# A hybrid decoder layer on one core: transposed attention weights through two PSUM regions, and a new order of work on ScalarE and VectorE

## Chip, core and metric

The kernel runs on one core of a Trainium2 chip. The metric is device time in microseconds (us). Matrix products run on TensorE (PE in the profile; PEld is its weight load), and the rest on VectorE (DVE), ScalarE (ACT), GpSimd (POOL) and the DMA queues.

## What is computed

One decoder layer for 1024 prompt tokens and 8 sequences of 4 new tokens: four mixers after one input projection, an output projection, a gated MLP, a gated embedding. The two attention mixers matter here:

```python
s = einsum('bqhd,bsd->bqhs', qi, ki); score = einsum(relu(s), wi) * IDX_SCALE
_, sel = lax.top_k(score, n_sel)                                   # "dsa": the 256 best keys
a = softmax(q @ k[sel] * 64**-0.5); y_c = a @ v[sel]
a = softmax(q1 @ k1 * 32**-0.5) - lam * softmax(q2 @ k2 * 32**-0.5)  # "diff"
y_d = rmsnorm(a @ v) * (1 - lam_init)
```

## The kernel before

The attention is cut into items, one for each query tile i (128 tokens) and head h: "diff" and "dsa" for the prompt, "sdiff" and "sdsa" for the new tokens. `ITEMS` lists them in order; position n in it is called step n, and each step has four places p = 0 to 3. Between the pieces of an item, each engine does its share of "dense" work: the projections, and from step 37 the MLP of the first 384 tokens, at a fixed number of products for each place. Steps 39 to 62 hold the diff items of tiles 3 to 7, with an sdiff item after each of the first four tiles (steps 43, 48, 53, 58), and steps 63 to 86 the dsa items. In steps 39 to 60 there also runs the search for the 256th largest score, bit by bit: in a stage, VectorE forms a candidate (L1338), then VectorE counts three arrays (L1288) and ScalarE three others (L1357), and VectorE's next stage begins by reading both (L1324). Most stages stand at places 1 and 3 up to step 49, at 2 and 3 in steps 52 and 53, and at 1 and 2 in steps 55 to 59.

An item goes through these pieces. Step n, place 0: PE makes the logits (L1507, sdiff L1517), VectorE adds the mask and takes the maximum (`dve_maxima`, L1787, L1796; ends with L1805), ScalarE takes the exponentials (`act_exp`, L1644). Place 3: VectorE combines the two maps (`dve_finish`, L1814 to L1817). Step n+1, places 2 and 3: PE transposes the weights in chunks of up to four 128-column blocks (`pe_transposes`, L1578, sdiff L1582) into PSUM bank 4, and ScalarE copies each chunk out (`act_transposed`, L1687, sdiff L1689). Step n+2, place 1: PE multiplies by the values (`pe_outputs`, L1550) into bank 5, whose halves serve two tiles in turn. Once a tile has its four heads, VectorE reads it at step n+3, place 0 (`dve_tile`, L1844 to L1850, with a power on POOL, L1944), PE transposes the result at n+4, place 1 (L1602), and ScalarE copies it (L1674).

All uses of bank 4 stand in one list, `USES`: chunks ("tr"), a tile's result ("y"), products for the samples ("so", transposed back as "sot", L1594) and some small ones. PE may write for use k only when ScalarE has copied use k-1:

```python
def pe_use(pe, use):
    k = USE_OF[use]
    if k:
        pe.wait_ge(use_cp, k)
```

ScalarE at a step: place 0 the exponentials of n; place 1 copies of sample and tile results, then its counts; place 2 the first chunk of n-1, then counts; place 3 the second chunk, then counts. VectorE: place 0 `dve_tile(n-3)` and maxima; places 1 and 2 stages; place 3 `dve_finish`, then a stage. The dense pieces (gate's tanh L905 on ScalarE, its product L958 on VectorE, the MLP sum L950 on VectorE) stand between them. Weights are fetched by SP's queue.

Of the kernel before, what the change touches and what calls it, by code (L numbers as in the profile page):

```python
# [7 lines left out]
P = 128  # L8
# [356 lines left out]
def chunks(n):  # L365
    kind, i, h = ITEMS[n]
    return {"none": 0, "sdiff": 2, "sdsa": 1}.get(kind, (i + 4) // 4)
# [6 lines left out]
USES = []  # L374
for n in range(NN):
    if n >= 2 and ITEMS[n - 2][0] in ("sdiff", "sdsa"):
# [8 lines left out]
USE_OF = {use: k for k, use in enumerate(USES)}  # L385
TR_OF = {use: sum(a[0] != "so" for a in USES[:k]) for k, use in enumerate(USES)}


def build(nc, d):
# [4 lines left out]
    with ExitStack() as ctx:  # L394
# [123 lines left out]
        def bank(j):  # L518
            return ps8[:, j]

# [219 lines left out]
        def tile_no(n):  # L740
            return sum(item[0] in PROMPT for item in ITEMS[:n]) // 4

# [351 lines left out]
        def pe_use(pe, use):  # L1094

            k = USE_OF[use]
            if k:
                pe.wait_ge(use_cp, k)

        def pe_misc(pe, use):  # L1100
            pe_use(pe, use)
            kind = use[0]
            if kind == "v":
# [3 lines left out]
                for j, slot in enumerate((DV, DV + 1, CV)):  # L1107
                    last = nc.tensor.transpose(bank(4)[0:w, j * P:(j + 1) * P], Z[:, slot, cols], c_("ident"))
            if kind == "maps":
# [5 lines left out]
                last = nc.tensor.matmul(bank(4)[:, 0:w], early_("maps")[:, c * P:(c + 1) * P], H[:, PV + c, cols], start=True, stop=True)  # L1115
            if kind == "wcol":
                pe.wait_ge(s_early, 16)
                for g in range(2):
                    last = nc.tensor.matmul(bank(4)[:, 8 * g:8 * g + 8], early_(f"e{g}", NS), ctok[0:NS, QT, HD:HD + 8], start=True, stop=True)
            if kind == "dsum":  # L1120
                pe.wait_ge(dsq, 1)
                last = nc.tensor.matmul(bank(4)[:, 0:64], c_("headones"), osqs[:, :], start=True, stop=True)
            last.then_inc(tr_mm, 1)

        def act_misc(act, use):
            kind = use[0]
            act.wait_ge(tr_mm, TR_OF[use] + 1)
            if kind == "v":
                t = use[1]
                w = P if t < QT else NS  # L1130
                nc.scalar.activation(dtok[0:w, t], bank(4)[0:w, 0:256], ACT.Copy)
                last = nc.scalar.activation(ctok[0:w, t], bank(4)[0:w, 256:328], ACT.Copy)
            if kind == "maps":
                c, half = use[1:]
                cols = part_a if half == 0 else slice(NA + (half - 1) * CB, NA + half * CB)
                last = nc.scalar.activation(H[:, PV + c, cols], bank(4)[:, 0:cols.stop - cols.start], ACT.Copy, scale=p_("pool_scale")[:, c:c + 1])
            if kind == "wcol":
                last = nc.scalar.activation(wcp, bank(4)[:, 0:16], ACT.Copy)
            if kind == "dsum":
                last = nc.scalar.activation(omean[:, :], bank(4)[:, 0:64], ACT.Identity, bias=eps[:, :], scale=1.0 / HD)  # L1140
# [396 lines left out]
        def pe_outputs(pe, n):  # L1537
# [3 lines left out]
            pe.wait_ge(use_cp, USE_OF["tr", n, chunks(n) - 1] + 1)  # L1541
            pt = probs_t(n)
            if kind in PROMPT:
                tile = tile_no(n)
                if h == 0 and tile:
                    pe.wait_ge(o_read, tile)
                for b in range(i + 1):
                    v = dtok[:, b, HD * h:HD * h + HD] if kind == "diff" else ctok[:, b, 0:HD]
                    at = 256 * (tile % 2) + HD * h
                    last = nc.tensor.matmul(bank(5)[:, at:at + HD], pt[:, b * P:(b + 1) * P], v, start=b == 0, stop=b == i)  # L1550
            else:
                pe_use(pe, ("so", n))
                if kind == "sdiff":
                    pe.wait_ge(dv_in, 16 * 2 * NPG * (i + 1))
                    for g in range(NPG + 1):
                        rows = P if g < NPG else NS
                        for b in range(2):
                            v = pair_values[b][:, g] if g < NPG else dtok[0:NS, QT, 0:256]
                            last = nc.tensor.matmul(bank(4)[32 * b:32 * b + 32, 0:256], pt[0:rows, g * 64 + 32 * b:g * 64 + 32 * b + 32], v,
                                                    start=g == 0, stop=g == NPG)  # L1560
                for c in range(2 if kind == "sdsa" else 0):
                    for g in range(NPG + 1):
                        rows = P if g < NPG else NS
                        v = dsa_values(i, c)[:, g] if g < NPG else ctok[0:NS, QT, 0:HD]
                        out, p = bank(4)[0:HD, c * 16:c * 16 + 16], pt[0:rows, g * 32 + c * 16:g * 32 + c * 16 + 16]
# [3 lines left out]
        def pe_transposes(pe, n, c):  # L1569
# [5 lines left out]
            pe_use(pe, ("tr", n, c))  # L1575
            if kind in PROMPT:
                for b in range(4 * c, min(4 * c + 4, i + 1)):
                    last = nc.tensor.transpose(bank(4)[:, (b % 4) * P:(b % 4 + 1) * P], logits(n)[:, b * P:(b + 1) * P], c_("ident"))  # L1578
            elif kind == "sdiff":
                for g in (range(5, NPG + 1) if c else range(5)):  # L1580
                    w = P if g < NPG else NS
                    last = nc.tensor.transpose(bank(4)[0:w, (g - 5 * c) * 64:(g - 5 * c) * 64 + 64], logits(n)[0:64, g * P:g * P + w],  # L1582
                                               c_("ident", 64)[:, 0:64])
            else:
                for g in range(NPG + 1):
                    w = P if g < NPG else NS
                    last = nc.tensor.transpose(bank(4)[0:w, g * 32:g * 32 + 32], logits(n)[0:32, g * P:g * P + w], c_("ident", 32)[:, 0:32])
            last.then_inc(tr_mm, 1)

        def pe_sample_back(pe, n):  # L1590

            pe_use(pe, ("sot", n))
            for c in range(2):
                last = nc.tensor.transpose(bank(4)[:, 64 * c:64 * c + 64], so_rows[0:64, c * P:(c + 1) * P], c_("ident", 64)[:, 0:64])  # L1594
            last.then_inc(tr_mm, 1)

        def pe_tile(pe, n):
            if ends_tile(n):
                pe.wait_ge(yt_ready, tile_no(n) + 1)
                pe_use(pe, ("y", n))  # L1600
                for j in range(2):
                    last = nc.tensor.transpose(bank(4)[:, j * P:(j + 1) * P], yt[:, j * P:(j + 1) * P], c_("ident"))  # L1602
# [30 lines left out]

        def act_exp(act, n):
# [12 lines left out]
        def act_sample(act, n):  # L1647
# [4 lines left out]
            if kind == "sdiff":  # L1652
                last = nc.scalar.activation(so_rows[0:64, :], bank(4)[0:64, 0:256], ACT.Copy)
            else:
                o = bank(4)[0:HD, 0:32].rearrange("p (b h t) -> p h b t", b=2, h=4)
# [5 lines left out]
        def act_sample_back(act, n):  # L1661
# [3 lines left out]
                                 bank(4)[:, 0:128].rearrange("p (c b r) -> p c b r", c=2, b=2), ACT.Copy).then_inc(use_cp, 1)  # L1665
# [1206 lines left out]
```

## Time and profile before

| | |
|---|---|
| three runs | 1782.15, 1775.49, 1781.06 us; median 1781.06 |
| span of the profiled execution | 1784.0 us |
| PE busy | 1641.7 us (92%) |
| VectorE busy | 1120.8 us (63%) |
| ScalarE busy | 684.7 us (38%) |
| GpSimd busy | 215.2 us (12%) |

No time outside the span is given for the profiled execution, so its span is its time here; it lies 2.9 us above the median of the runs. An engine's share is an average over stages with different limits, so the stretches of the span are to be read one by one. A row's arrow names what the idle time before an instruction ended on; "issue" is idle time for which the profile shows no wait.

### The profile page before, as it was taken

What the parts mean: (1) busy time and instruction counts of PE and PEld (TensorE: products, weight loads), DVE (VectorE), ACT (ScalarE), POOL (GpSimd) and SP (SyncE); (2) the same over time, 40 slices, a digit from 0 to 9 for tenths busy, and PEclk for the clock granted to TensorE, in tenths of its full rate; (3) what the DMA queues carried; (4) which work ended last, traced back from release to release, by engine and by line L of the source; (5) the groups of instructions that cost most, each with busy time, mean ns of one, the idle gap of its engine ahead of it and who ended that gap; (6) DMA issues with size and microseconds to landing.
All of it is one profiled execution on the core that took longest, in us unless ns stands there. A gap on an engine that the chain in (4) does not pass through costs nothing.

```text
span 1784.0 us, 26755 instructions
## 1 busy us (share of the span) xinstructions
PE 1641.7 (92%) x9433; PEld 1400.4 (78%) x9433; DVE 1120.8 (63%) x2415; ACT 684.7 (38%) x1273; POOL 215.2 (12%) x360
## 2 busy tenths in 40 slices
PE   6989998998978798889999999999999999999996
PEld 5978898873534454456787799899999999999995
DVE  6466856277788887776656555566555555556845
ACT  5333443354367366532333333342222222222531
POOL 1000000031313322063322001000000000000000
PEclk9999999998989898899998999999999999999997
DMA  5331122141523323132322223122222222222312
GB/s 192 118 106 48 60 78 72 62 160 61 175 74 118 104 92 107 49 106 94 92 75 73 72 83 138 53 83 86 72 71 71 71 71 71 71 71 77 106 60 110
DMA packets 52815, 158.32 MB, mean 89 GB/s; under 512 B 9776, under 2 KB 13872, under 8 KB 52704
## 3 DMA queue, kind: packets, MB, share of 16 engines
q1 hardware_dynamic: 37840, 121.37, 20.2%
q0 software_dynamic: 14864, 35.53, 6.3%
q8 instruction: 62, 1.02, 0.2%
q14 instruction: 49, 0.40, 0.1%
HBM read 147.10 MB, written 9.76 MB: 88 GB/s over the span
## 4 chain that ended last, share of the span: by engine, by line
PE 57%; DVE 11%; issue 8%; ACT 5%; POOLq 1%; POOL 1%; DMA 0%; DVEq 0%; ACTq 0%
PE ps L2077 22%; PE ps L832 15%; PE ps L2264 9%; ACT act_junk L1357 2%; PE ps L1550 2%; DVE junk_b L1288 2%; DVE Pb_b L1787 2%; PE ps L1507 1%; PE ps L2438 1%; PE ps L1578 1%; PE ps L1162 1%; DVE SC L1194 1%; ACT Pb_b L1644 1%; DVE wl L581 1%; ACT wh L574 1%
## 5 line engine op out<-in xcount | busy, mean ns | idle before, releaser
L581 DVE TENSOR_TENSOR wl<-wr,wh 128x1024 fp32r<-128x1024 f32 x176 | 215.4, 1224 | 284.0 <-ACT wh L574 283.4
L574 ACT ACTIVATE wh<-wr 128x1024 fp32r<-128x1024 f32 x176 | 186.0, 1057 | 424.0 <-PE ps L2077 221.1
L2077 PE MATMUL ps<-xh_b,wh 128*128 128x336 f32 x960 | 305.4, 318 | 7.4 <-DVE wl L581 3.3
L2077 PE MATMUL ps<-xl_b,wh 128*128 128x336 f32 x960 | 305.7, 318 | 0.0
L2077 PE MATMUL ps<-xh_b,wl 128*128 128x336 f32 x960 | 303.9, 317 | 0.0
L2077 PEld LDWEIGHTS ps<-xh_b,wh 128*128 128x128 f32 x960 | 181.8, 189 | 8.9 <-DVE wl L581 4.0
L2077 PEld LDWEIGHTS ps<-xh_b,wl 128*128 128x128 f32 x960 | 181.8, 189 | 0.0
L2077 PEld LDWEIGHTS ps<-xl_b,wh 128*128 128x128 f32 x960 | 181.3, 189 | 0.0
L832 PE MATMUL ps<-x_a,wr 128*128 128x384 f32 x384 | 152.9, 531 | 1.7 <-DVE H L950 1.7
L832 PE MATMUL ps<-xh_a,wh 128*128 128x384 f32 x400 | 141.2, 353 | 8.3 <-ACT Z L873 3.0
L1644 ACT ACTIVATE Pb_b<-Pb_b,tiny 128x512 f32<-128x512 f32 (+6 forms) x68 | 65.2, 959 | 201.2 <-DVE tiny L1805 201.2
L832 PE MATMUL ps<-xl_a,wh 128*128 128x384 f32 x400 | 139.4, 349 | 0.0
L832 PE MATMUL ps<-xh_b,wh 128*128 128x336 f32 x352 | 114.9, 326 | 0.8 <-ACT Z L873 0.8
L832 PE MATMUL ps<-xl_b,wh 128*128 128x336 f32 x352 | 115.2, 327 | 0.0
L832 PE MATMUL ps<-xh_b,wl 128*128 128x336 f32 x352 | 114.5, 325 | 0.0
L1288 DVE TENSOR_SCALAR_CACHE_REDUCE junk_b<-SC,tk_b 32x1056 uint16<-32x1056 uint16 (+7 forms) x105 | 107.5, 1024 | 6.8 <-DMA SC<-score_spill 3.3
L2264 PE MATMUL ps<-al_b,wh 128*128 128x336 f32 x352 | 111.6, 317 | 0.0
L2264 PE MATMUL ps<-ah_b,wh 128*128 128x336 f32 x352 | 111.3, 316 | 0.2 <-DVE H L2348 0.2
L2264 PE MATMUL ps<-ah_b,wl 128*128 128x336 f32 x352 | 111.3, 316 | 0.0
L832 PEld LDWEIGHTS ps<-x_a,wr 128*128 128x128 f32 x384 | 71.1, 201 | 50.0 <-issue 19.3
L2348 DVE TENSOR_TENSOR H<-H,ps 128x336 f32<-128x336 f32 x176 | 85.1, 502 | 33.2 <-PE ps L2264 31.4
L1357 ACT ACTIVATE act_junk<-SC,tk_b 128x1024 bf16<-128x1024 uint16 (+2 forms) x93 | 93.4, 1004 | 9.9 <-DVE tk_b L1338 7.4
(420 smaller groups left out, 3174.1 us busy)
## 6 DMA issues: line engine op xcount, KB each, us to landing
wr<-in_weights SPq DMA_DIRECT2D x212, 512.0 KB, 3.4
pages<-in_d_pages POOLq DMA_DIRECT2D x64, 128.0 KB, 2.4
values<-in_d_pages POOLq DMA_DIRECT2D x64, 128.0 KB, 2.4
pages<-in_c_pages POOLq DMA_DIRECT2D x128, 32.0 KB, 2.1
H<-in_xT SPq DMA_DIRECT2D x8, 336.0 KB, 8.6
H<-in_xT POOLq DMA_DIRECT2D x8, 336.0 KB, 5.8
out_y<-Y_out_b SPq DMA_DIRECT2D x8, 336.0 KB, 2.3
H<-in_xT SPq DMA_DIRECT2D x8, 192.0 KB, 4.9
```

The source lines that it names most:

```text
L574: nc.scalar.activation(wh[:, slot], wr[:, slot], ACT.Copy).then_inc(w_hi, 1)
L581: nc.vector.tensor_tensor(wl[:, slot], wr[:, slot], wh[:, slot].bitcast(f32), ALU.subtract).then_inc(w_lo, 1)
L832: last = nc.tensor.matmul(out[:, cols], w, x, start=j == 0, stop=j == count - 1)
L1162: last = nc.tensor.matmul(bank(2 * (u % 2) + h)[:, 0:w], Z[r, QI + p, i * P:(i + 1) * P], Z[r, KI2, a:a + w], start=True, stop=True)
L1288: return nc.vector.tensor_scalar(self.junk[0:rows, 0:S], src, scalar, 0.0, op, ALU.add, accum_out=self.col(CNT, j, rows))
L1357: nc.scalar.activation(out[:, 0:S], self.half(j, k >= 15), ACT.Sign, bias=self.col(NBIAS, j), accum_out=self.col(CNT, j)).then_inc(self.ac ...
L1550: last = nc.tensor.matmul(bank(5)[:, at:at + HD], pt[:, b * P:(b + 1) * P], v, start=b == 0, stop=b == i)
L1644: last = nc.scalar.activation(p, p, ACT.Exp, bias=nm[0:rows, col:col + 1], scale=SCALE[kind], accum_out=sm[0:rows, col:col + 1])
L1787: last = nc.vector.tensor_tensor_reduce(out=logits(n, m)[:, 0:S], in0=src[:, 0:S], in1=mask, scale=1.0, scalar=-3e38, op0=ALU.add, op1=ALU ...
L2077: last = nc.tensor.matmul(bank(first_bank + c)[:, 0:CB], w, x, start=k == 0 and t == 0, stop=k == KC - 1 and t == 2)
L2264: last = nc.tensor.matmul(down_bank(v), w, x, start=q == 0 and t == 0, stop=q == 1 and t == 2)
L2348: nc.vector.tensor_tensor(cols, cols, down_bank(v), ALU.add).then_inc(h_ffn, 1)
```

## The change

Tiles 6 and 7 are transposed in three chunks of 4, 2 and 2 (or 1) blocks; tiles 4 and 5 stay at two. The uses are sorted into two kinds. "Narrow" ones (so, y, wcol, dsum, and every second chunk) go to the upper half of bank 5, and the others stay in bank 4. A use waits for the previous use of its own kind. Values products now use only the lower half of bank 5, and since PE must not write a bank while another engine reads it, a narrow use also waits until VectorE has read all tiles multiplied before it, and values products wait until earlier narrow uses are copied. `pe_outputs` waits chunk by chunk. The third chunk is transposed and copied at the end of place 3, after the dense work. On ScalarE, the exponentials move from place 0 to place 2, behind the copy of the first chunk. On VectorE, `dve_tile` (and POOL's power) moves from place 0 of the third step to place 2 of the second, ahead of that place's stage, and at place 3 the stage comes before `dve_finish`.

```diff
-    return {"none": 0, "sdiff": 2, "sdsa": 1}.get(kind, (i + 4) // 4)
+    return {"none": 0, "sdiff": 2, "sdsa": 1}.get(kind, 1 if i < 4 else 2 if i < 6 else 3)
+
+def blocks(n, c):
+    i = ITEMS[n][1]
+    return range(*((0, min(4, i + 1)), (4, min(6, i + 1)), (6, i + 1))[c])
...
-        USES += [("tr", n - 1, c) for c in range(chunks(n - 1))]
+        USES += [("tr", n - 1, c) for c in range(min(2, chunks(n - 1)))]
     if n >= 2 and ITEMS[n - 2][0] == "sdiff":
         USES.append(("sot", n - 2))
+    if n >= 1 and chunks(n - 1) == 3:
+        USES.append(("tr", n - 1, 2))
...
+def narrow(use):
+    return use[0] in ("so", "y", "wcol", "dsum") or use[0] == "tr" and use[2] == 1
...
+        def use_at(use):
+            return ps8[:, 5, 256:512] if narrow(use) else ps8[:, 4]
...
         def pe_use(pe, use):
-            k = USE_OF[use]
-            if k:
-                pe.wait_ge(use_cp, k)
+            if BEFORE[use] >= 0:
+                pe.wait_ge(use_cp, BEFORE[use] + 1)
+            read = tiles_before(use) if narrow(use) else 0
+            if read:
+                pe.wait_ge(o_read, read)
...
         # pe_outputs
+                if NARROW_BEFORE[n]:
+                    pe.wait_ge(use_cp, NARROW_BEFORE[n])
                 for b in range(i + 1):
+                    for c in range(chunks(n)):
+                        if b == blocks(n, c)[0]:
+                            pe.wait_ge(use_cp, USE_OF["tr", n, c] + 1)
...
         # act_mixers
             if p == 0:
-                act_exp(act, n)
...
                 if n:
                     act_transposed(act, n - 1, 0)
+                act_exp(act, n)
                 act_stage(act, n, 2)
...
         # dve_mixers
             if p == 0:
-                if n >= 3:
-                    dve_tile(dve, link, n - 3)
                 dve_maxima(dve, link, n)
...
             if p == 2:
+                if n >= 2:
+                    dve_tile(dve, link, n - 2)
                 dve_stage(dve, link, n, 2)
...
             if p == 3:
+                dve_stage(dve, link, n, 3)
                 dve_finish(dve, link, n)
-                dve_stage(dve, link, n, 3)
...
         # scalar; the same with pe_transposes on PE
                 act_dense(act, place)
+                if place % 4 == 3 and third_chunk(place // 4):
+                    act_transposed(act, place // 4 - 1, 2)
```

## Rows read from the trace of the kernel before

**Rows 1.** The page: span, and busy time of each engine.

```profile
span 1784.0 us, 26755 instructions
PE 1641.7 (92%) x9433; PEld 1400.4 (78%) x9433; DVE 1120.8 (63%) x2415; ACT 684.7 (38%) x1273; POOL 215.2 (12%) x360
```

**Rows 2.** Windows: length; PE, PEld, DVE, ACT, POOL busy (count); granted clock; DMA; GB/s.

```profile
0.00:450.00 450.00, 403.72 (x2325) 348.26 (x2325) 275.77 (x699) 189.84 (x376) 40.88 (x71) 0.97 0.29 97
...
510.00:767.00 257.00, 213.66 (x919) 115.09 (x920) 204.25 (x509) 142.97 (x290) 61.59 (x110) 0.89 0.29 94
767.00:1062.00 295.00, 274.82 (x1558) 219.92 (x1557) 175.68 (x355) 107.57 (x206) 76.13 (x120) 0.95 0.25 78
...
522.00:528.00 6.00, 6.00 (x15) 2.85 (x14) 5.06 (x14) 3.71 (x8) 0.61 (x1) 0.50 0.01 3
```

**Rows 3.** Waits of PE, 510 to 767 us: total, times, longest.

```profile
PE ps L1582 <- ACT PT_b L1689: 17.7, 4, 8.8
PE ps L1578 <- ACT PT_b L1687: 11.8, 8, 3.2
PE ps L1578 <- ACT H L1674: 6.7, 2, 4.9
PE ps L1594 <- ACT PT_b L1687: 4.6, 4, 3.1
```

**Rows 4.** Waits of PE, 767 to 1062 us.

```profile
PE ps L832 <- issue: 10.9, 9, 3.2
PE ps L1578 <- ACT H L1674: 5.5, 1, 5.5
```

**Rows 5.** Waits of PE, 0 to 450 us.

```profile
PE ps L1578 <- ACT H L1674: 2.5, 2, 1.8
```

**Rows 6.** Waits of VectorE, 510 to 767 us.

```profile
DVE tk_b L1324 <- ACT act_junk L1357: 13.4, 9, 2.7
DVE gv_a L958 <- ACT ge_a L905: 8.7, 5, 2.4
DVE Pb_b L1796 <- PE ps L1517: 5.8, 2, 3.1
...
DVE Pb_b L1787 <- PE ps L1507: 4.3, 1, 4.3
...
DVE tiny L1814 <- ACT Pb_b L1644: 2.0, 1, 2.0
DVE H L950 <- PE ps L832: 1.9, 1, 1.9
```

**Rows 7.** Timeline of step 51: start, duration, instruction, idle before it.

```profile
618.34 0.17 DVE L1805 TENSOR_SCALAR tiny<-tiny 128x2 f32<-128x2 f32 x1
618.54 0.93 ACT L1644 ACTIVATE Pb_b<-Pb_b,tiny 128x768 f32<-128x768 f32 x1 [9.52 <-DVE tiny L1805]
...
620.39 0.51 ACT L905 ACTIVATE ge_a<-gv_a 128x384 f32<-128x384 f32 x1
620.80 0.60 ACT L1674 ACTIVATE H<-ps,subln 128x128 f32<-128x128 f32 x2
...
621.55 1.09 PE L1578 MATMUL ps<-cst,Pb_b 128*128 128x128 f32 x4 [4.93 <-ACT H L1674]
```

**Rows 8.** Timeline of step 44, sdiff transposed.

```profile
520.15 0.75 DVE L1288 TENSOR_SCALAR_CACHE_REDUCE junk_b<-SC,tk_b 128x512 uint16<-128x512 uint16 x1
...
521.02 0.42 ACT L1689 ACTIVATE PT_b<-ps 128x320 f32<-128x320 f32 x1
...
521.49 0.68 PE L1582 MATMUL ps<-cst,Pb_b 64*128 64x64 f32 x4 [8.75 <-ACT PT_b L1689]
```

**Rows 9.** Groups by shape: count, busy, mean ns, idle before.

```profile
L1687 ACT ACTIVATE PT_b<-ps 128x256 f32<-128x256 f32 x8 | 3.0, 378 | 7.3 <-PE ps L1578 7.3
L1844 DVE TENSOR_TENSOR ot<-ps,tiny 128x256 f32<-128x256 f32 x8 | 3.3, 416 | 0.0
L1817 DVE SCALAR_TENSOR_TENSOR Pb_b<-Pb_b,tiny 128x768 f32<-128x768 f32 x4 | 4.1, 1019 | 0.1
```

**Rows 10.** Timeline: a stage at place 3, read after `dve_finish` (step 52).

```profile
638.32 0.17 DVE L1324 TENSOR_TENSOR tk_b<-tk_b 128x12 f32<-128x12 f32 x1 [1.51 <-ACT act_junk L1357]
```

**Rows 11.** Timeline: a weight load after a wait already met.

```profile
651.33 0.94 PEld L832 LDWEIGHTS ps<-gu_a,wr 128*128 128x128 f32 x4 [0.55 <-issue]
```

More of the change, by code:

```diff
@@ L381 @@
     if n >= 1:
-        USES += [("tr", n - 1, c) for c in range(chunks(n - 1))]
+        USES += [("tr", n - 1, c) for c in range(min(2, chunks(n - 1)))]
     if n >= 2 and ITEMS[n - 2][0] == "sdiff":
         USES.append(("sot", n - 2))
+    if n >= 1 and chunks(n - 1) == 3:
+        USES.append(("tr", n - 1, 2))
 USE_OF = {use: k for k, use in enumerate(USES)}
+def narrow(use):
+    return use[0] in ("so", "y", "wcol", "dsum") or use[0] == "tr" and use[2] == 1
+BEFORE = {use: max((j for j in range(k) if narrow(USES[j]) == narrow(use)), default=-1) for k, use in enumerate(USES)}
+NARROW_BEFORE = {n: sum(1 for use in USES[:k] if narrow(use)) and 1 + max(j for j in range(k) if narrow(USES[j])) for n, k in USES_BEFORE.items()}
 TR_OF = {use: sum(a[0] != "so" for a in USES[:k]) for k, use in enumerate(USES)}
@@ L741, in tile_no, with tiles_before @@
             return sum(item[0] in PROMPT for item in ITEMS[:n]) // 4
+        def tiles_before(use):
+            k = USE_OF[use]
+            return tile_no(1 + max(n for n, first in USES_BEFORE.items() if first <= k))
         def diff_tiles(n):
@@ L1114, in pe_misc @@
                 w = cols.stop - cols.start
-                last = nc.tensor.matmul(bank(4)[:, 0:w], early_("maps")[:, c * P:(c + 1) * P], H[:, PV + c, cols], start=True, stop=True)
+                last = nc.tensor.matmul(use_at(use)[:, 0:w], early_("maps")[:, c * P:(c + 1) * P], H[:, PV + c, cols], start=True, stop=True)
             if kind == "wcol":
@@ L1575, in pe_transposes @@
             pe_use(pe, ("tr", n, c))
+            dst = use_at(("tr", n, c))
             if kind in PROMPT:
-                for b in range(4 * c, min(4 * c + 4, i + 1)):
-                    last = nc.tensor.transpose(bank(4)[:, (b % 4) * P:(b % 4 + 1) * P], logits(n)[:, b * P:(b + 1) * P], c_("ident"))
+                for at, b in enumerate(blocks(n, c)):
+                    last = nc.tensor.transpose(dst[:, at * P:(at + 1) * P], logits(n)[:, b * P:(b + 1) * P], c_("ident"))
             elif kind == "sdiff":
@@ L1581, in pe_transposes @@
                     w = P if g < NPG else NS
-                    last = nc.tensor.transpose(bank(4)[0:w, (g - 5 * c) * 64:(g - 5 * c) * 64 + 64], logits(n)[0:64, g * P:g * P + w],
+                    last = nc.tensor.transpose(dst[0:w, (g - 5 * c) * 64:(g - 5 * c) * 64 + 64], logits(n)[0:64, g * P:g * P + w],
                                                c_("ident", 64)[:, 0:64])
@@ L1586, in pe_transposes @@
                     w = P if g < NPG else NS
-                    last = nc.tensor.transpose(bank(4)[0:w, g * 32:g * 32 + 32], logits(n)[0:32, g * P:g * P + w], c_("ident", 32)[:, 0:32])
+                    last = nc.tensor.transpose(dst[0:w, g * 32:g * 32 + 32], logits(n)[0:32, g * P:g * P + w], c_("ident", 32)[:, 0:32])
             last.then_inc(tr_mm, 1)
@@ L1632, in pe_mixers, with third_chunk @@
                     pe_sample_back(pe, n - 2)
+        def third_chunk(n):
+            return n >= 1 and chunks(n - 1) == 3
         def act_exp(act, n):
@@ L1839, in dve_tile @@
             heads = lambda x: x.rearrange("p (h d) -> p h d", d=HD)
-            o = heads(bank(5)[:, 256 * (tile % 2):256 * (tile % 2) + 256])
+            o = heads(bank(5)[:, 0:256])
             a = 4 * (tile % 2)
@@ L2696, in _ @@
                 pe_dense(pe, place)
+                if place % 4 == 3 and third_chunk(place // 4):
+                    pe_transposes(pe, place // 4 - 1, 2)
             pe_out(pe)
```

61 lines of the change are left out of this document (31 added, 30 removed).

## The prediction

> **What bounds the kernel now.** I read the page first: PE is busy 92% of the span, no other engine more than 63% [rows 1]. That average hides different stages, so I cut the span into windows [rows 2]. From 0 to 450 us and from 1062 us on, the change touches little. Between 510 and 767 us, where the search runs beside the diff items, PE is busy 213.7 of 257 us although its mean granted clock is only 0.89, and VectorE 204.3 us. Neither is full: the two hold each other up. From 767 to 1062 us PE is busy 274.8 of 295 us and sets the pace.
>
> Then I read the waits. In the search stretch PE waits 17.7 us for the first sdiff chunk's copy, 11.8 us for a first prompt chunk's, 6.7 us for a tile's, 4.6 us before the samples are transposed back: 40.8 us, all for ScalarE to empty bank 4 [rows 3]. The timeline of step 51 shows why ScalarE is late. It meets the exponentials first and stands before them for 9.52 us until VectorE's maxima; then they take 1.85 us (618.54 to 620.39), then come tanh and the tile's copy; PE has idled 4.93 us [rows 7].
>
> But PE's idle time is not the price. VectorE is nearly a second bound here, and PE, freed, meets it again. So I cost this stretch by VectorE's waits: 13.4 us for ScalarE's counts, 8.7 us for tanh, 5.8 and 4.3 us for logits from a late PE, 2.0 us for exponentials, 1.9 us for the MLP product [rows 6].
>
> **The change part by part, search stretch.**
>
> *ScalarE's counts before the exponentials.* In steps with a stage at place 1, ScalarE now counts at once instead of 1.85 us later [rows 7]. Of nine waits totalling 13.4 us, seven are in such steps, and I take 1 us from each: 7 us gained. Bounds: nothing, and all 13.4 us.
>
> *Tanh not behind the exponentials.* Tanh stands directly behind them in steps 44 and 51 ([rows 7] shows the second). Two of the five waits, each near the longest, 2.4 us [rows 6], go: 4.6 us. Bounds 0 and 8.7.
>
> *PE no longer waits for bank 4.* The second chunk and the tile's result have a region of their own, so the 11.8 and 6.7 us [rows 3] go, and the samples' way back waits only for the first chunk: most of 4.6 us. What VectorE gets of these 23 us is its waits for logits, 5.8 and 4.3 us, and for the MLP product, 1.9 us: 12.0 us in all [rows 6]. The stalls ahead are about as long (longest 3.2, 3.1 and 4.9 against 3.1, 4.3 and 1.9), so I take 10.7. Bounds 0 and 12.0.
>
> *The sdiff stall of 17.7 us mostly stays.* At the step after an sdiff item, a tile has just been multiplied. The sdiff second chunk is narrow, so PE must wait for VectorE to read that tile, at place 2, behind the stage of place 1. In step 44 that stage's last count starts at 520.15 and takes 0.75 us, so the read (0.416 us [rows 9]) would end near 521.4; ScalarE's copy today frees PE at 521.49, after 8.75 us [rows 8]. The wait changes its name. It costs VectorE nothing, as VectorE is the one that is late. I take no gain. The Trainium skill ("PSUM — Partial Sum Buffer", PSUM bank collisions) says that PSUM must be guarded by bank and quadrant, not by address, because engines in disjoint columns of one bank collide; by that rule these waits can't be left out, and by a guard on addresses alone the 17.7 us of PE would go too. No row shows a collision.
>
> *`dve_finish` behind the stage.* Finishing now waits for nothing at step 50: 2.0 us gained [rows 6]. But in steps 52 and 53, with stages at places 2 and 3, finishing stood between VectorE's counts and its wait for ScalarE's. Even so 1.51 us were left to wait [rows 10]. Without that cover its time, 1.0 us for the combination [rows 9] and some 0.5 us of small operations, is waited: 2 x 1.6 = 3.2 us lost. ScalarE's tanh of step 53 now stands behind exponentials started later: 1.5 us lost. Combined weights come up to one stage later at steps 44 to 53, but PE uses them two places into the next step.
>
> *`dve_tile` moved.* The same five operations and POOL's power, once a tile: nothing. At place 2 it waits for PE's place 1, where PE is mostly ahead.
>
> *Third chunks.* 16 more copies at no more than 0.378 us [rows 9]: 6 us on ScalarE, busy 143 of 257 us [rows 2], hidden. Should that cover go, they cost 6 us.
>
> Sum here: 7 + 4.6 + 10.7 + 2.0 - 3.2 - 1.5 = 19.6 us gained.
>
> **From 767 us.** At 773 us PE waits 5.5 us for a tile's copy [rows 4], the tile ending in step 58, and from there PE sets the pace: this goes entirely. PE's clock had dropped to 0.50 after such a stall, with PE then busy throughout (522 to 528 us [rows 2]); a few us of work at half speed go too, 1.5 us. Gain 7.0. The other large wait there, 10.9 us on dense products [rows 4], is about operands, which the change leaves.
> New waits: values products of tiles 4 to 7 stop for the second and third chunk, 24 times among the dsa items (8 once, 8 twice). Met waits elsewhere delay a weight load by up to 0.55 us while PE's products go on [rows 11]; so between 0 and 13 us; I take 0.1 us each, 2.4, as products are queued ahead. After each dsa tile PE's second chunk waits for VectorE's read, four times, behind one mask stage at place 1; PE has two places of dense work before it. Between 0 and 1.0 us each; I take 0.5, 2 us in all.
>
> **Before 450 us.** Of two waits of 2.5 us for a tile's copy [rows 5], all goes; with small ones, 3 us. PE sets the pace there.
>
> **Total.** 19.6 + 7.0 + 3 - 2.4 - 2 = 25.2 us from the profiled 1784.0 us: 1758.8. That execution lies 2.9 us above the median of the runs, so I predict 1756 us, a ratio of 0.986.
>
> **The rivals.**
>
> *More than that, 1730 (chance 0.10).* With 23 of 40.8 us of stalls gone, PE hardly drops to the low clock, and pulls VectorE along. At a mean clock of 0.89, PE spends 22% of 257 us, 57 us, at half speed [rows 2]; half of that time is loss. If most of it matters, 25 us more. Against it: VectorE's 204 us plus its own latencies leave it little room.
>
> *VectorE is the bound and nothing comes back but the edge, 1774 (0.19).* PE runs ahead, then waits for maxima, or for values' chunks, and ScalarE's counts at place 2 are now behind the exponentials, so VectorE waits there instead. Then 19.6 shrinks to about 0, and 7.0 + 3 - 4.4 = 5.6 remain, within half a per cent of no change. For it: the sdiff case above, where one wait takes another's place. Against it: after the stage at place 2, VectorE still has finishing and the next maxima to do before it reads ScalarE's counts.
>
> *Slower, 1796 (0.12).* The place is `dve_finish` behind the stage at place 3. Combined weights come later by VectorE's counts, some 3.6 us, in about ten steps; where PE already stands at the transposes, it idles for as long and its clock then falls to 0.50 as it did at 522 us [rows 2]. Ten such stalls with as much lost again at half speed are 70 us of PE's time; PE has 257 - 213.7 = 43.3 us of idle time to lend [rows 2], of which about 15 stay in the sdiff stalls, so 42 us of loss less the 25 gained. It decides once PE arrives less than 3.6 us after finishing, in half or more of the steps. The Trainium skill ("TensorE: Matmul & The Clock Gate", Part 1) says that throttled is the default state and only activity releases it; by that rule each new long stall is followed by slow products, as at 522 us, and this case would give the 1796.
> Against it: PE reaches the transposes two places into the next step, and today waits there for ScalarE, hardly ever for VectorE.
>
> *The forecast, 1756 (0.59).* Its own range, from the bounds: 1742 to 1768.
>
> **How the numbers follow.** Half a per cent is 9 us, about what a measurement of this kernel can tell from no change. The forecast and the first rival are faster by more than that, and a little of the second: 0.59 + 0.10 + 0.02 = 0.71. Same: 0.17 of the second and a little of the slow case, 0.18. Slower: 0.11. The range for 8 in 10 leaves out the slow case's greater part and most of the first rival: 1738 to 1785.
>
> **What would show it.** L1578 waits for PT_b and for H gone from PE's list between 510 and 767 us; L1582 waiting about as long, now for VectorE (ot, L1844's successor); VectorE's wait for ScalarE's counts at 6 to 7 us instead of 13.4; that stretch shorter by some 20 us; no stall of PE near 773 us; mean clock above 0.89. It is wrong if PE's waits for combined weights grow past 10 us, if VectorE waits for exponentials or counts as long as before, or if values products show gaps between chunks.

## Result, and the profile after

| | before | changed |
|---|---|---|
| median of the runs on the same chip | 1780.65 us | 1756.46 us |
| lowest and highest | 1775.49, 1782.15 | 1745.55, 1759.72 |
| profiled execution | 1784.0 (its span) | 1758.01 (span 1756.3) |

The ratio is 0.987, 95% interval 0.9834 to 0.9906: faster, by 24 us or 1.3%, with the whole interval below 1. I had predicted 1756 us. The total is right. The working is only partly so. In the search stretch two of its terms missed by more than 3 us each and cancelled each other, and terms were added up that don't add. Behind the search a gain was foretold that didn't come. This is the more useful part of what follows.

The page of the changed kernel, beside [rows 1]: PE and VectorE have as many entries as before, and ScalarE has 16 more, the third chunks.

```profile
span 1756.3 us, 26856 instructions
PE 1630.0 (93%) x9433; PEld 1393.2 (79%) x9433; DVE 1121.2 (64%) x2415; ACT 682.9 (39%) x1289; POOL 214.2 (12%) x360
```

Windows of the changed kernel, columns as in [rows 2]. The last line is the search stretch by its own landmarks, from VectorE's first decision for the samples and tile B (L1367, 488.3 us) to the value found (L1408, 728.1 us).

```profile
0.00:450.00 450.00, 407.50 (x2345) 349.25 (x2346) 278.19 (x703) 190.37 (x378) 41.74 (x73) 0.97 0.30 98
510.00:767.00 257.00, 228.87 (x1017) 127.11 (x1018) 215.98 (x535) 152.15 (x321) 73.23 (x131) 0.93 0.33 103
767.00:1062.00 295.00, 272.47 (x1579) 224.71 (x1578) 174.27 (x335) 103.87 (x204) 69.85 (x110) 0.95 0.28 89
488.00:728.00 240.00, 207.63 (x921) 113.68 (x920) 208.72 (x536) 150.32 (x312) 57.71 (x103) 0.93 0.31 99
```

The same stretch in the kernel before (L1338 at 494.9 us to L1379 at 754.3 us):

```profile
495.00:754.00 259.00, 213.93 (x916) 114.86 (x916) 208.14 (x532) 151.48 (x306) 58.18 (x103) 0.89 0.28 91
```

A fixed window such as 510 to 767 us misleads once the program has shifted: it now holds work that lay behind 767 us. Cut at landmarks, VectorE does the same 208 us of work in 240 us instead of 259. PE's busy time shrank, from 213.9 to 207.6 us, with as many products: at a granted clock of 0.93 instead of 0.89 less of its work ran at the lower of its two levels. The stretch is 19.6 us shorter in this pair of traces, and I had forecast 19.6; over two traces of each kernel (below) it is 18.5.

Waits of PE in the changed kernel, 488 to 728 us, beside [rows 3]:

```profile
PE ps L1617 <- ACT PT_b L1728: 6.4, 1, 6.4
PE ps L1617 <- DVE ot L1883: 6.1, 2, 3.5
PE ps L859 <- DVE H L977: 4.2, 3, 2.3
PE ps L1613 <- ACT so L1703: 3.9, 1, 3.9
PE ps L1617 <- DVE Pb_b L1866: 3.4, 2, 2.6
```

L1613 and L1617 are L1578 and L1582 of before. The waits of L1578 for the chunk copies and for the tile's copy, 11.8 and 6.7 us, are gone. The sdiff waits stand where I expected them, under another name: 12.5 us instead of 17.7. The one put down to ScalarE is of this kind too. Timeline around 511 us (step 44):

```profile
511.11 0.17 DVE L1375 TENSOR_SCALAR tk_b<-tk_b 128x12 f32<-128x12 f32 x1
511.19 0.42 DVE L1883 TENSOR_TENSOR ot<-ps,tiny 128x256 f32<-128x256 f32 x1
...
511.31 0.42 ACT L1728 ACTIVATE PT_b<-ps 128x320 f32<-128x320 f32 x1
...
511.75 0.66 PE L1617 MATMUL ps<-cst,Pb_b 64*128 64x64 f32 x4 [6.41 <-ACT PT_b L1728]
```

VectorE's read of the tile ends at 511.61, ScalarE's copy at 511.73, so the view names the copy. But that copy empties the other bank, and by the code PE's second chunk doesn't wait for it; the narrow use before it, the result of a tile multiplied many steps earlier, is long over. What holds PE is the read, behind a stage, as in [rows 8]. A wait that ends on two things at nearly the same time has to be read in the code.

Waits of VectorE, same stretch, beside [rows 6]:

```profile
DVE tk_b L1353 <- ACT act_junk L1386: 10.5, 8, 3.5
...
DVE Pb_b L1826 <- PE ps L1536: 3.5, 1, 3.5
DVE gv_a L985 <- ACT ge_a L932: 2.0, 3, 1.1
DVE Pb_b L1835 <- PE ps L1546: 1.0, 1, 1.0
```

Before, between the same landmarks (495 to 754 us), the waits for counts have this line, and the others are as in [rows 6]:

```profile
DVE tk_b L1324 <- ACT act_junk L1357: 14.5, 10, 2.7
```

That is 14.5 for counts, 8.7 for tanh, 4.3 and 5.8 for logits, 1.9 for the MLP product, 2.0 for exponentials, 37.2 us in all. Now 17.0. The 20.2 us of VectorE's waits that are gone account for the 19.6 us.

Step 52, where finishing no longer covers VectorE's wait for counts ([rows 10] has 1.51 there):

```profile
619.76 0.17 DVE L1353 TENSOR_TENSOR tk_b<-tk_b 128x12 f32<-128x12 f32 x1 [3.48 <-ACT act_junk L1386]
```

Waits behind the search. First VectorE, 745 to 981 us:

```profile
DVE tiny L1859 <- ACT Pb_b L1683: 27.3, 9, 5.3
DVE H L977 <- PE ps L859: 16.4, 11, 5.4
DVE Pb_b L1826 <- PE ps L1536: 12.8, 8, 3.4
DVE Pb_b L1835 <- PE ps L1562: 8.6, 3, 5.1
DVE wl L603 <- ACT wh L596: 6.7, 5, 3.6
```

And of the kernel before over the same work, 771 to 1009 us:

```profile
DVE Pb_b L1787 <- PE ps L1507: 22.7, 9, 6.4
DVE wl L581 <- ACT wh L574: 16.3, 5, 6.1
DVE H L950 <- PE ps L832: 12.5, 10, 3.2
...
DVE tiny L1820 <- ACT Pb_b L1644: 2.5, 3, 1.0
```

Then PE, 745 to 1045 us, beside [rows 4]:

```profile
PE ps L859 <- issue: 15.8, 10, 4.6
```

VectorE waited 2.5 us for exponentials and now 27.3; its waits for logits (22.7 to 12.8) and for the high halves of the weights (16.3 to 6.7) shrank by 19.5 us together. PE's 5.5 us for the tile's copy are gone, and its idle time in dense products is up from 10.9 to 15.8.

### The profile page after: what moved, and what is told of

It reads as the page before. It is cut to its first block, busy times and chain, and to the rows that moved or that the text cites. A ratio compares the mean times of both kernels' runs of the same rounds, so it can differ in the third digit from the quotient of the medians.

```text
span 1756.3 us, 26856 instructions
## 1 busy us (share of the span) xinstructions
PE 1630.0 (93%) x9433; PEld 1393.2 (79%) x9433; DVE 1121.2 (64%) x2415; ACT 682.9 (39%) x1289; POOL 214.2 (12%) x360
## 4 chain that ended last, share of the span: by engine, by line
PE 72%; DVE 14%; issue 6%; ACT 6%; DMA 1%; POOL 0%; SPq 0%; DVEq 0%; POOLq 0%; ACTq 0%
PE ps L859 26%; PE ps L2116 22%; PE ps L2303 9%; DVE junk_b L1317 3%; PE ps L1582 2%; PE ps L1536 2%; ACT act_junk L1386 2%; PE ps L1613 1%; DVE Pb_b L1826 1%; PE ps L1191 1%; DVE wl L603 1%; PE ps L2477 1%; ACT wh L596 1%; DVE SC L1223 1%; PE ps L1593 1%
## 5 line engine op out<-in xcount | busy, mean ns | idle before, releaser
L859 PEld LDWEIGHTS ps<-xh_a,wh 128*128 128x128 f32 x400 | 75.9, 190 | 21.9 <-issue 15.0
```

The source lines that it names most:

```text
L859: last = nc.tensor.matmul(out[:, cols], w, x, start=j == 0, stop=j == count - 1)
```

## The experiments

I cut every trace at the same four landmarks: VectorE's first decision (L1338), the value found (L1379), the last start of the samples' dsa logits (L1533) and the end. In the changed kernel these lines are L1367, L1408 and L1562. Times in us; the clock is that of the search stretch; the ratio is to the kernel before, on the same chip.

| kernel | to first decision | search | clock | found to last logits | rest | median | ratio, 95% |
|---|---|---|---|---|---|---|---|
| before, first trace | 494.9 | 259.4 | 0.89 | 254.9 | 774.8 | 1780.65 | |
| before, again | 489.6 | 257.2 | 0.91 | 254.3 | 772.3 | 1775.68 | 0.9989 [0.9971, 1.0007] |
| changed, first trace | 488.3 | 239.8 | 0.93 | 253.5 | 774.7 | 1756.46 | 0.987 [0.9834, 0.9906] |
| changed, again | 487.4 | 239.8 | 0.93 | 257.1 | 774.6 | 1757.36 | 0.9871 [0.9844, 0.9899] |
| VectorE's order only | 491.7 | 255.3 | 0.92 | 262.4 | 772.2 | 1780.27 | 1.0011 [0.9996, 1.0027] |
| exponentials moved only | 484.9 | 248.5 | 0.92 | 260.6 | 773.7 | 1774.38 | 0.9993 [0.9977, 1.001] |
| both orders, one bank | 484.7 | 241.7 | 0.94 | 252.9 | 774.8 | 1758.88 | 0.990 [0.9873, 0.9927] |
| changed, exponentials back | 489.2 | 245.3 | 0.91 | 249.8 | 773.0 | 1762.62 | 0.9925 [0.9901, 0.9949] |
| changed, finishing first | 484.2 | 254.7 | 0.90 | 253.5 | 773.7 | 1765.6 | 0.9944 [0.9913, 0.9974] |
| changed, one wait for all chunks | 484.4 | 238.0 | 0.93 | 252.2 | 774.8 | 1755.08 | 0.9874 [0.9846, 0.9903] |
| changed, tile read at place 1 | 482.6 | 237.0 | 0.91 | 256.8 | 774.8 | 1758.15 | 0.989 [0.9867, 0.9913] |
| changed, dsa exponentials first | 481.4 | 233.6 | 0.95 | 252.1 | 773.0 | 1748.52 | 0.9847 [0.9817, 0.9878] |
| changed, dsa exponentials first, again | 487.2 | 236.8 | 0.94 | 252.0 | 773.1 | 1748.35 | 0.9832 [0.9805, 0.986] |
| changed, tile read at place 1 and dsa exponentials first | 482.5 | 237.0 | 0.91 | 256.6 | 772.0 | 1752.06 | 0.9861 [0.983, 0.9892] |

One profiled execution isn't the median. That of "exponentials moved only" was the fastest of its 12 runs (1769.34), that of "VectorE's order only" the slowest of its 12 (1783.3), that of the first "dsa exponentials first" the fastest of its 6 (1741.75). So a difference of 5 us between two single traces says nothing alone; differences in the search stretch are firmer, since the same code repeats it within 0.0 to 3.2 us in the three pairs above; but a difference of 2 or 3 us between single traces says nothing there either.

The granted clock of the whole execution is on record for every run, and most of the spread within a kernel goes with it. The kernel before took 1782.6 us at 0.963, 1777.3 to 1777.7 at 0.969 and 1769.75 at 0.974, all on one chip. So kernels are compared below by their medians and, where it matters, at equal clock as well.

### Both kernels again

The changed kernel:

> The changed kernel as it is, as the yardstick for the three beside it on the same chip. All theories: ratio 0.987 to the kernel before, between 0.983 and 0.991, some 23 us.

The kernel before, no edit:

> The kernel before, once more, for a second trace. My account says that the stretch ahead of 450 us gave about 7 to 10 us, more than the 3 us of PE's waits that the change could remove there; in the one trace of before the first scoring product of the samples starts at 450.4 us, in seven traces of changed kernels between 436.8 and 444.6 us. If the account is right, the second trace has it at 447 to 453 us again. Rival: that trace happened to be slow there, and the second one has it at 438 to 445 us. From the first decision of the search to the found value both expect 259 us, within 3 us. Ratio 0.998 to 1.002 for both.

The changed kernel repeats at 1757.36 us (0.9871), and the kernel before stands at a ratio of 0.9989 to itself, with 1 in its interval. Its second trace has the first scoring product of the samples at 445.0 us, at the upper edge of the rival's 438 to 445; the first had 450.4. So part of the 6.6 us by which the first pair of traces differed ahead of the search was chance. With two traces each, the change gives 4.4 us there (492.3 against 487.9), less than the 5.3 us between the two traces of the kernel before, 18.5 in the search (258.3 against 239.8), and nothing that shows behind it: from the value found to the end 1029.7 and 1026.6 us before, mean 1028.2; 1028.2 and 1031.7 changed, mean 1030.0.

### Which part gives the search its 18.5 us

```diff
 # both orders, one bank: on the kernel before (POOL's power moves with the tile read)
             if p == 0:
-                act_exp(act, n)
...
                     act_transposed(act, n - 1, 0)
+                act_exp(act, n)
...
             if p == 0:
-                if n >= 3:
-                    dve_tile(dve, link, n - 3)
...
             if p == 2:
+                if n >= 2:
+                    dve_tile(dve, link, n - 2)
                 dve_stage(dve, link, n, 2)
...
-                dve_finish(dve, link, n)
                 dve_stage(dve, link, n, 3)
+                dve_finish(dve, link, n)
```

> The kernel before with both new orders (ScalarE's exponentials at place 2; VectorE's tile read at place 2 and stage before finishing at place 3) but the one bank 4 for all uses, two chunks at most and both halves of bank 5. Theory of the prediction: of the gain, 10 us or so came from a PE no longer waiting for the bank, the rest from the orders: ratio 0.991 to 0.995, 9 to 16 us won. Rival: once ScalarE's copies come ahead of the exponentials the second region is not needed: ratio 0.985 to 0.989, as good as the whole change.

The first two hunks alone (exponentials moved only):

> The kernel before with only ScalarE's order changed: exponentials at place 2, behind the copy of the first chunk; one bank, VectorE's order as before. Theory of the prediction: counts and tanh come earlier and PE gets its first chunk's copy ahead of the exponentials, so most waits of PE of 17.7 and 11.8 us shrink; but VectorE's finishing at place 3 waits for exponentials. 5 to 15 us won, ratio 0.992 to 0.997. Rival: the wait for exponentials takes all of it: ratio 0.998 to 1.005.

The others alone (VectorE's order only):

> The kernel before with VectorE's and POOL's order alone changed (tile read at place 2 of the second step, stage ahead of finishing at place 3); the exponentials stay at place 0, one bank. Theory: the two moves need each other. VectorE doesn't wait for late exponentials here, so its own reordering gives little: search stretch 255 to 260 us against 259 us, ratio 0.995 to 1.000. Rival: VectorE's order is what gains, and the exponentials' move only needs it: search stretch at 250 us or less, ratio 0.993 or lower.

And the changed kernel with the first two undone (exponentials back at place 0, two banks):

> The changed kernel with only ScalarE's order undone: all exponentials at place 0 again. Theory of the prediction: the freed bank alone lets PE ahead but ScalarE's counts, tanh and copies stand behind the exponentials again; of the 27.7 us won between the traces, 7 + 4.6 us for counts and tanh, 2 for the late exponentials' cover, and the tiles' copies are lost, so the ratio to the kernel before is 0.992 to 0.997 (6 to 14 us won instead of 23). Rival: the gain is the bank's alone, because PE's stalls were what counted; then the ratio stays at 0.985 to 0.989.

The orders without the second region give 0.990, between the two expectations and as far from one as from the other. The exponentials back at place 0 give 0.9925, as my account expected. One order without the other gives nothing in the median: 0.9993 and 1.0011. VectorE's waits in the search stretch show part of the reason. Exponentials moved only, 485 to 733 us:

```profile
DVE tiny L1814 <- ACT Pb_b L1644: 11.5, 7, 2.3
DVE Pb_b L1787 <- PE ps L1507: 6.3, 1, 6.3
DVE tk_b L1324 <- ACT act_junk L1357: 5.2, 6, 2.0
...
DVE gv_a L958 <- ACT ge_a L905: 2.2, 3, 1.0
```

VectorE's order only, 492 to 747 us:

```profile
DVE tk_b L1324 <- ACT act_junk L1357: 16.2, 9, 2.5
DVE gv_a L958 <- ACT ge_a L905: 6.0, 5, 2.4
DVE Pb_b L1796 <- PE ps L1517: 5.9, 2, 3.1
...
DVE Pb_b L1787 <- PE ps L1507: 2.9, 1, 2.9
```

Both orders, one bank, 485 to 726 us:

```profile
DVE tk_b L1324 <- ACT act_junk L1357: 7.7, 8, 3.4
DVE Pb_b L1787 <- PE ps L1507: 6.3, 1, 6.3
...
DVE Pb_b L1796 <- PE ps L1517: 2.9, 2, 1.5
DVE gv_a L958 <- ACT ge_a L905: 2.2, 3, 1.3
```

Moving the exponentials shortens the waits for counts and tanh, but VectorE, still finishing first, meets the late exponentials seven times (11.5 us). With VectorE's new order that meeting is gone; while the exponentials are early there is nothing to remove.

That the exponentials' move alone ends with so little in its median, though its search stretch was some 10 us shorter in the trace, goes with the clock. On the same chip its 12 runs were granted 0.959 to 0.967, median 0.963, and the kernel before 0.962 to 0.974, median 0.970. At 0.963 the move's five runs took 1772.7 to 1775.3 us, and the one of the kernel before 1782.6. So it gained some 7 to 10 us that a lower clock took back. Why its clock is lower isn't shown. VectorE's order alone has no such gain: at 0.968 it took 1778.7 to 1780.0 us, the kernel before 1776.1 to 1779.1.

The two-bank part can now be read in two ways. Among kernels with VectorE's new order:

| | exponentials at place 0 | at place 2 |
|---|---|---|
| one bank | 1.0011 (search 255.3) | 0.990 (241.7) |
| two banks | 0.9925 (245.3) | 0.987 (239.8) |

With the exponentials in their old place the second region gives 10.0 us in the search; with them moved, 1.9. In the first case VectorE's waits for logits and for the MLP product fall from 10.0 us (5.9, 2.9 and 1.2) to this, between 489 and 735 us with the exponentials back:

```profile
DVE Pb_b L1835 <- PE ps L1546: 1.0, 1, 1.0
```

In the second they fall from 9.2 to 4.5, and the waits for counts rise from 7.7 to 10.5. Both edits help PE past the same thing, a ScalarE that stands before exponentials while PE waits for a copy, and in the search stretch the second to be made finds less left.

The 1.9 us come from one trace of the kernel with one bank and lie within what a repeat differs by, so they are not a price. The ratios, 0.990 and 0.987, are 5 us apart, and their intervals overlap. At equal clock, though on different chips, the distance can be larger: at 0.973 the kernel with one bank took 1761.3 us and the changed kernel 1752.1; at 0.969, 1760.1 and, in its first set of runs, 1758.0. The runs with one bank had the higher clock, 0.969 to 0.978 against 0.966 to 0.974. Behind the search, PE was idle for 20.4 us with one bank and for 17.7 and 17.1 with two, between the value found and the last logits. What the second region is worth behind the orders is therefore known only as something between nothing and 9 us.

PE's waits in "both orders, one bank" show what it still stands for with one bank, 28.2 us in all, in a search stretch only 1.9 us longer:

```profile
PE ps L1582 <- ACT PT_b L1689: 10.7, 3, 6.4
PE ps L1578 <- ACT PT_b L1687: 9.0, 7, 1.7
PE ps L1594 <- ACT PT_b L1687: 8.5, 3, 5.1
```

### Finishing behind the stage

```diff
 # finishing first: on the changed kernel
-                dve_stage(dve, link, n, 3)
                 dve_finish(dve, link, n)
+                dve_stage(dve, link, n, 3)
```

> The changed kernel with only VectorE's order at place 3 undone: finishing before the stage. Theory of the prediction: putting the stage first won 2.0 us at step 50 and lost 3.2 us at steps 52 and 53, so undoing it changes little, within 2 us, towards faster. Rival: with the exponentials at place 2, finishing first stands waiting for them in every step, and 8 to 20 us are lost.

It loses 0.7% (0.9944 against 0.987), the rival's case. Waits of VectorE and the window of its search stretch, 484 to 739 us:

```profile
DVE tiny L1853 <- ACT Pb_b L1683: 19.7, 6, 6.4
DVE tk_b L1353 <- ACT act_junk L1386: 5.7, 6, 2.7
```

```profile
484.00:739.00 255.00, 212.69 (x920) 117.47 (x919) 208.61 (x537) 150.12 (x311) 57.87 (x103) 0.90 0.30 93
```

19.7 us of waits for exponentials come, 4.8 of waits for counts go (5.7 against 10.5), and the stretch is 14.9 us longer, as much as the difference of the two. The edit that I had costed as a loss of 3.2 us less a gain of 2.0 is worth 14.9 us here. How much it is worth depends on the rest again: with one bank and the old place of the tile read, finishing first and late exponentials had a stretch of 248.5 us, 6.8 longer than with both orders. Whether the second region or the tile read makes finishing first dearer isn't shown.

### The new waits of the values products, and the tile read

```diff
 # one wait for all chunks: on the changed kernel, pe_outputs
+                pe.wait_ge(use_cp, USE_OF["tr", n, chunks(n) - 1] + 1)
...
-                    for c in range(chunks(n)):
-                        if b == blocks(n, c)[0]:
-                            pe.wait_ge(use_cp, USE_OF["tr", n, c] + 1)
```

> The changed kernel, but the values products of an item wait once, for all chunks, ahead of the first product. Theory of the prediction: the 24 waits inside dsa items cost 0.1 us each, so 2 to 3 us are won. Rival: a wait that is met costs nothing there, as PE has products queued; the time stays within 1 us, or rises by up to 2 us where the first chunk is there before the last.

```diff
 # tile read at place 1: on the changed kernel, VectorE (POOL alike)
             if p == 1:
+                if n >= 2:
+                    dve_tile(dve, link, n - 2)
                 dve_stage(dve, link, n, 1)
...
             if p == 2:
-                if n >= 2:
-                    dve_tile(dve, link, n - 2)
                 dve_stage(dve, link, n, 2)
```

> The changed kernel, but VectorE reads a finished tile at place 1, ahead of that place's stage, instead of at place 2. Theory of the prediction: PE's stalls on the sdiff second chunk (6.4 and 6.1 us) are waits for that read and fall below 4 us in all, but VectorE sets the pace there, so the time changes by less than 3 us. Rival: PE's stalls count, for they also lower its clock, and 6 to 12 us are won. A second rival: VectorE now waits for the values products at place 1 and a stage starts later, and 2 to 5 us are lost.

The chunk waits cost nothing that can be measured, the rival's case: 0.9874 against 0.9871. With the tile read ahead of the stage, PE's list for 483 to 720 us has

```profile
PE ps L859 <- DVE H L977: 7.2, 3, 4.1
PE ps L1593 <- ACT PT_b L1731: 4.1, 2, 3.5
...
PE ps L1617 <- DVE Pb_b L1866: 3.4, 2, 2.6
PE ps L1617 <- DVE ot L1883: 2.9, 1, 2.9
```

The 6.4 us put down to ScalarE's copy are gone with a move of VectorE's read alone, as the code has it. 12.5 us of stalls became 2.9; PE's waits on other rows grew by 3.0 for the MLP sum and 2.8 for the samples' values products (L1593); and the time stayed (0.989 against 0.9871), as my account expected. PE's idle time in the search stretch as a whole fell only from 32.4 to 29.2 us (a rough figure, as its list has 887 entries of PE and the other 921), so most of the stall came back on other rows; what a PE that is really freed would give isn't tested by this run.

### Exponentials first again in the dsa steps

```diff
 # on the changed kernel, act_mixers
             if p == 0:
+                if n >= DSA_B:
+                    act_exp(act, n)
...
-                act_exp(act, n)
+                if n < DSA_B:
+                    act_exp(act, n)
```

`DSA_B` is the first dsa step, 63.

> The changed kernel, but for the dsa and sdsa items (steps 63 on) the exponentials stand at place 0 again. Theory of the prediction: what was lost after 779 us (4.5 us between two landmarks of the traces) is waits of PE in the values products and for the tiles' read, so this changes nothing (within 1 us) and VectorE's new wait for exponentials is harmless. Rival: VectorE, which now waits 31.4 us for exponentials between 745 and 1045 us, brings its dense operands late, and PE's wait on dense products rose from 10.9 to 15.8 us for that; then this wins 4 to 5 us over the changed kernel, and the waits of VectorE's reciprocal fall below 5 us.

> The same kernel as e1_dsa_exp_first, timed in more rounds. Theory: VectorE's 24 us of waits for exponentials in the dsa stretch only moved to later waits (for logits, and for ScalarE in the projections), so the exponentials back at place 0 there give at most 3 us: ratio 0.985 to 0.989. Rival: they give 5 us or more over the changed kernel: ratio 0.984 or lower.

1748.52 and 1748.35 us, against 1757.36 and 1756.46 for the changed kernel: by the ratios 0.2 to 0.4% better, though each interval still overlaps that of the changed kernel. Both times the ratio speaks for the rival: the first (0.9847) is not the nothing that the prediction's account gives, and the second (0.9832) lies on the rival's side of 0.984, so my second account, at most 3 us, is too low as well. Waits of VectorE, 741 to 976 us of the second trace:

```profile
DVE Pb_b L1829 <- PE ps L1536: 18.2, 8, 5.8
DVE H L977 <- PE ps L859: 16.4, 10, 5.2
DVE wl L603 <- ACT wh L596: 13.9, 5, 5.0
```

The 27.3 us for exponentials are gone. 5.4 us are back in the waits for logits (12.8 to 18.2), and 7.2 in those for ScalarE's share of the weights' splitting (6.7 to 13.9). In the traces the part from the value found to the last logits is 252.1 and 252.0 us against 253.5 and 257.1, and the rest 773.0 and 773.1 against 774.7 and 774.6: 3.3 and 1.6 us, 4.9 in all. The medians differ by 8 to 9. The rest goes with the clock: the median of the runs was granted 0.972 with this edit and 0.969 without. At 0.974 the edit's runs took 1746.4 and, on another chip, 1744.3 us, the changed kernel 1750.9; at 0.966, 1757.4 against 1760.6 and 1761.3. So I take 3 to 7 us as the edit's. Whether the higher clock is the edit's or chance stays open, as the search stretch also differs (233.6 and 236.8 against 239.8) though this edit doesn't touch its steps.

Tile read at place 1 and dsa exponentials first, both on the changed kernel:

> The changed kernel with exponentials at place 0 for the dsa items and the tile read at place 1 ahead of the stage. Candidate for a better version. Theory: each alone measured within 4 us of the changed kernel, and neither removes a wait that sets the pace, so together 0 to 5 us: ratio 0.984 to 0.989. Rival: with no late tile read and no late exponentials both gains add up, 8 us or more: ratio 0.983 or lower.

0.9861 [0.983, 0.9892]: the theory's range, no better than the dsa edit alone. That one, the changed kernel with the exponentials at place 0 from step 63 on, is the best version found: some 1748.4 us, a ratio of 0.983 to 0.985 to the kernel before.

## Why the prediction was right, and where it was not

**Bound and place.** VectorE was costed as the pace of the search stretch, by its waits and not by PE's 40.8 us of stalls. The runs bear this out. VectorE's work there is 208 to 209 us in all of them. Since both landmarks are VectorE's, the length is then that work plus its waits in any case, and this alone proves nothing; what counts is that PE's stalls don't give the length. With both orders and one bank, PE stands 28.2 us for bank 4 and the stretch is 241.7 us; with two regions it stands 12.5 us for the tile read and 4.7 for copies, and the stretch is 239.8. Moving the tile read takes 9.6 us of PE's stalls on those rows away, and the median stays.

**Counts, 7 gained, and 3.2 lost in steps 52 and 53.** Net 3.8 foretold, 4.0 measured (14.5 to 10.5). The loss in step 52 is 2.0 us (1.51 to 3.48) against 1.6 foretold; step 53 has no such wait. The sign that I gave for this term, a wait of 6 to 7 us, left my own 3.2 us of loss out, and was missed.

**Tanh, 4.6 gained, 1.5 lost.** Net 3.1 foretold, 6.7 measured. The foretold loss in step 53 didn't come, and the waits that don't stand directly behind exponentials fell too.

**Exponentials, 2.0.** Right in size, wrong in weight. I read the order of finishing and stage as a small trade. Undone in the changed kernel, it costs 14.9 us in the search, because the exponentials now end late in the step. I had priced the order with the exponentials where they stood before, and my pricing of their move left out what VectorE's finishing would then meet.

**PE no longer waits for bank 4, 10.7.** This is the term that was sized worst. VectorE's waits for logits and for the MLP product fell by 7.5 us in the changed kernel, 12.0 to 4.5. So this kind of wait was priced 3.2 us too high and tanh 3.6 us too low, and that the total of 19.6 came out is in part luck.

The step behind it was to price each edit against the kernel before and add up. A single price for the region doesn't exist: it is 10.0 us in the search with the exponentials at place 0, close to my 10.7, and 1.9 in the trace with them moved. Taken last, the region leaves 16.6 us to the orders (258.3 to 241.7), against 7 + 4.6 + 2.0 - 3.2 - 1.5 = 8.9 foretold. Taken between VectorE's order and the exponentials it leaves them 8.5 (3.0 and 5.5). So the two parts of the sum come out about right for one order of making the edits, and wrong by 8.8 and 7.7 us for the other. The region on the kernel before with neither new order wasn't run.

**The sdiff stall stays.** Right: 12.5 of 17.7 us remain as waits for VectorE's read, and the run that removes most of it shows no gain. No run leaves the wait out; PE could then write a bank while VectorE reads it. The Trainium skill ("PSUM — Partial Sum Buffer", PSUM bank collisions) wants that guard by bank; no trace here shows what happens without it.

**From 767 us, 7.0 gained, 4.4 lost.** Wrong on both sides. The 5.5 us stall did go, but PE then waits elsewhere: between the same points, 771 to 1009 us before and 745 to 981 after, it is idle for 14.5 and 16.2 us. The chunk waits and late tile reads for which I took 4.4 us cost nothing in the runs that change them. What I left out is VectorE before exponentials in the dsa steps, 2.5 us before and 27.3 after, which the text had named only as a sign of being wrong. With the dsa exponentials back at place 0, the part from the value found to the end is 1025.1 us in both traces, 3.1 less than before and near the 2.6 foretold, though the two traces of the kernel before differ by as much. For the change itself the two traces each give 1028.2 before and 1030.0 changed: nothing, within what two traces can tell.

**Before 450 us, 3.** Measured 4.4 up to the first decision, by two traces each; the two traces of the kernel before differ by 5.3 there, so this confirms nothing. The tile-copy waits of [rows 5] are gone in the changed kernel, and in the one with the exponentials moved alone 0.2 us of them is left; so their going is the order's, not the second region's.

**The rivals.** "Nothing comes back but the edge" had in its favour that one wait takes another's place: this is what happened in the dsa steps, not in the search. Two of the rivals' times don't follow from their own terms: 5.6 us off 1781 are 1775.5, not 1774, and 42 us of loss less 25 gained make 1798, not 1796. The slower case asked for PE to stand at the transposes for VectorE's combined weights. It did so for 1.8 us in the prompt's items, as before, and for 3.4 instead of 0.8 in the sdiff items. The Trainium skill ("TensorE: Matmul & The Clock Gate", Part 1) has throttling as the default that activity lifts. The traces agree in direction for this pair: in the search stretch of the two kernels, idle time fell from 45 to 32 us (259 - 213.9, 240 - 207.6), and the granted clock rose from 0.89 to 0.93. They don't for every pair: with the tile read at place 1 the idle time was 29 us or less and the clock 0.91. So idle time alone doesn't foretell the clock here, and no run shows what does.

## What to carry to other kernels

When several edits help the same late engine, their gains needn't add: price each one on top of the others, and ask which waits the first leaves for the second. An engine's order is worth what it meets on the other engines, so a reordering on ScalarE and one on VectorE may each show nothing in the median and together give one per cent; test them as a pair. Before calling an edit worth nothing, compare its runs with the others at the same granted clock. And cut traces at landmarks of the work: in a fixed window even the engine that sets the pace seems to work more.

## What was unexpected of the hardware

The same code takes different times with the clock it is granted, and a single trace can't tell this from an effect. Over the changed kernel's second set of runs, the mean clock went from 0.966 to 0.974 and the time from 1761.3 to 1750.9 us. From 744 us on, the two executions of the changed kernel took 236 and 240 us for the same dsa work. The windows of the first and the second trace:

```profile
745.00:981.00 236.00, 219.76 (x1210) 169.06 (x1210) 142.19 (x289) 86.56 (x177) 72.55 (x115) 0.95 0.26 80
```

```profile
744.00:984.00 240.00, 224.32 (x1210) 173.38 (x1210) 142.42 (x290) 86.65 (x177) 73.22 (x115) 0.93 0.25 79
```

PE's idle time is 16.2 and 15.7 us. The difference is all in its busy time, 219.8 and 224.3 us for the same 1210 entries, at a clock of 0.95 and 0.93. In the search stretch, where VectorE sets the pace, the same clock difference does less: with the tile read at place 1 it was 0.91 in a stretch of 237 us, shorter than the changed kernel's at 0.93.
